# First modulation divided between TensorE and VectorE, the first squares added up on VectorE, GpSimd's products by a scalar operand

## What is computed

```python
cond = jax.nn.silu(c)
for i in range(DEPTH):
    shift, scale, gate = jnp.split(cond @ ada_w[i] + ada_b[i], 3, axis=-1)
    h = rmsnorm(x, norm_g[i]) * (1 + scale[:, None, :]) + shift[:, None, :]
    ...                       # MLA, windowed or sparse attention of h
    x = x + gate[:, None, :] * y
```

## Time and profile before

| what | us |
|---|---|
| median of 3 runs | 3254.95 (3248.53 to 3257.18) |
| the profiled execution, its own time | 3258.99 |
| its span, first to last instruction | 3257.2 |
| TensorE busy | 3047.1 (94%) |
| VectorE busy | 996.4 (31%) |
| ScalarE busy | 643.2 (20%) |
| GpSimd busy | 884.9 (27%) |
| share of TensorE in the chain that ended last | 88% |

### The profile page before, as it was taken

How to read it: one execution, slowest core, us unless ns; L and a number is a source line. 1 busy time by engine, 2 the same in 40 slices (tenths; PEclk the granted TensorE clock), 3 DMA queues, 4 the chain that set the end, 5 groups by cost and what they waited for, 6 DMA issues and landing times.

```text
span 3257.2 us, 28075 instructions
## 1 busy us (share of the span) xinstructions
PE 3047.1 (94%) x10359; PEld 1693.3 (52%) x10359; DVE 996.4 (31%) x2032; ACT 643.2 (20%) x1452; POOL 884.9 (27%) x574
## 2 busy tenths in 40 slices
PE   8899989999999998998788978999999999999997
PEld 7465555575666644554456556444444444444443
DVE  2333354324455623335544254200000222100001
ACT  1232123222233412323323122100000100100000
POOL 5480480076350008406700000381000570000000
PEclk6999999989999999998899989999999999999999
DMA  6341341153231024223200200352222442222222
GB/s 220 99 144 62 110 136 39 54 155 106 71 91 33 14 79 138 88 72 101 77 17 13 59 6 26 116 169 89 77 71 72 152 157 65 68 74 76 78 71 70
DMA packets 267621, 278.08 MB, mean 85 GB/s; under 512 B 39379, under 2 KB 240352, under 8 KB 267392
## 3 DMA queue, kind: packets, MB, share of 16 engines
q1 hardware_dynamic: 238528, 175.56, 17.8%
q0 software_dynamic: 28224, 100.86, 9.9%
q10 hardware_dynamic: 768, 0.30, 0.0%
HBM read 274.59 MB, written 2.10 MB: 85 GB/s over the span
## 4 chain that ended last, share of the span: by engine, by line
PE 88%; DVE 7%; ACT 2%; DMA 2%; issue 1%; SPq 0%; DVEq 0%; ACTq 0%
PE psum L680 44%; PE psum L825 10%; PE psum L1277 9%; PE psum L1112 2%; PE psum L707 2%; PE psum L799 2%; PE psum L1143 2%; PE psum L1098 2%; PE psum L754 2%; PE psum L722 2%; PE psum L811 1%; PE psum L1148 1%; PE psum L949 1%; PE psum L950 1%; DVE probs L2012 1%
## 5 line engine op out<-in xcount | busy, mean ns | idle before, releaser
L680 PE MATMUL psum<-h,ring 128*128 128x512 f32 (+1 forms) x3216 | 1390.1, 593 | 28.8 <-ACT h L1412 27.1
L680 PEld LDWEIGHTS psum<-h,ring 128*128 128x128 f32 x3216 | 616.4, 193 | 764.4 <-issue 749.9
L607 POOL DMA_DIRECT2D ada_ring<-in_ada_w x192 | 113.0, 588 | 1775.8 <-DVE gains L1897 1504.2
L623 POOL TENSOR_TENSOR ada_sum<-ada_sum,ada_ring 128x1024 f32<-128x1024 f32 x168 | 396.9, 2363 | 14.1
L825 PE MATMUL psum<-og,ring 128*128 128x512 f32 x768 | 333.1, 593 | 2.3 <-DVE og L2430 2.0
L619 POOL TENSOR_TENSOR ada_ring<-ada_ring,cond 128x1024 f32<-128x1024 f32 x168 | 320.0, 1905 | 4.5 <-POOL ada_sum L623 1.6
L1277 PE MATMUL psum<-arena,ring 128*128 128x512 f32 x704 | 302.5, 592 | 0.0
L825 PEld LDWEIGHTS psum<-og,ring 128*128 128x128 f32 x768 | 144.6, 190 | 181.8 <-issue 178.3
L1277 PEld LDWEIGHTS psum<-arena,ring 128*128 128x128 f32 x704 | 133.8, 190 | 168.4 <-issue 168.4
L2440 DVE TENSOR_TENSOR arena<-psum,arena 128x512 f32 x44 | 30.4, 692 | 573.8 <-PE psum L680 573.8
L2059 DVE SCALAR_TENSOR_TENSOR x<-psum,mods,x 128x512 f32<-128x512 f32 x64 | 48.1, 751 | 481.3 <-PE psum L1277 272.2
(11 more groups left out here) (285 smaller groups left out, 2793.6 us busy)
## 6 DMA issues: line engine op xcount, KB each, us to landing
ada_ring<-in_ada_w POOLq DMA_DIRECT2D x192, 512.0 KB, 4.1
ring<-in_ffn_w_gate SPq DMA_DIRECT2D x22, 1024.0 KB, 5.3
ring<-in_ffn_w_up SPq DMA_DIRECT2D x22, 1024.0 KB, 5.3
ring<-in_ffn_w_down SPq DMA_DIRECT2D x32, 704.0 KB, 4.6
ring<-in_sc_w_in SPq DMA_DIRECT2D x12, 1024.0 KB, 6.1
ring<-in_mla_w_in SPq DMA_DIRECT2D x10, 1024.0 KB, 5.4
ring<-in_mla_w_out SPq DMA_DIRECT2D x8, 1024.0 KB, 5.2
ring<-in_swa_w_in SPq DMA_DIRECT2D x16, 512.0 KB, 5.2
```

What stands on the lines that cost most here:

```text
L607: pool.dma_start(ada_ring[:, i % 2, :], w[k * P:(k + 1) * P, first(part)]).then_inc(arrived[i % 2], n.give(f"ada_in{i % 2}", 16))
L623: step = nc.gpsimd.tensor_tensor(total, total, piece, ALU.add)
L680: m = pe.matmul(tile.at[:, part], lhs(k), rhs(k), start=(k == 0), stop=(k == K - 1))
```

## The change

It touches the start, and one instruction of GpSimd's later jobs:

- TensorE computes only weight tiles 1, 4 and 7 by one-column matmuls. Tiles 0, 2, 3, 5 and 6 are multiplied by `cond` and added up over the eight steps on VectorE (`first_sums`), into the still unused `ada_sum[:, 0:2048]`; each finished tile is summed over the partitions by TensorE with one matmul per column (`column_sums`), behind all direct tiles.
- GpSimd waits for all five sums of VectorE before its first fetch.
- The squares of `x` are added on VectorE between the copies (`add_square`), as in the later blocks; TensorE has two matmuls with ones behind the row groups in place of eight between the transposes.
- VectorE runs `normed(0)` before the rotary angle, and ScalarE the root and the shifts before the sines.
- GpSimd multiplies with `tensor_scalar` by a per-partition scalar in place of `tensor_tensor` with a broadcast operand, in all 192 steps.

```diff
+FIRST_ON_PE = (1, 4, 7)
...
             pool.wait_ge(S["cond_ready"], 1)
+            pool.wait_ge(S["first_summed"], FIRST_SLOTS - len(FIRST_ON_PE))
...
-                    step = nc.gpsimd.tensor_tensor(piece, ada_ring[:, i % 2, :], c.broadcast_to([P, CHUNK]), ALU.mult)
+                    step = nc.gpsimd.tensor_scalar(piece, ada_ring[:, i % 2, :], c, None, ALU.mult)
...
-                for i in range(FIRST_SLOTS):
+                for i in FIRST_ON_PE:
                     pe.wait_ge(S[f"first_in{i}"], 16)
                     for c in range(2):
                         for k in range(KT):
-                            m = pe.matmul(tile.at[:, 2 * i + c:2 * i + c + 1], w8(first_slots[i], P * c)(k), cond[:, k:k + 1],
-                                          start=(k == 0), stop=(k == KT - 1))
-                m.then_inc(S["tile_done"], 1)
+                            pe.matmul(tile.at[:, 2 * i + c:2 * i + c + 1], w8(first_slots[i], P * c)(k), cond[:, k:k + 1],
+                                      start=(k == 0), stop=(k == KT - 1))
+                summed = [i for i in range(FIRST_SLOTS) if i not in FIRST_ON_PE]
+                for at, i in enumerate(summed):
+                    pe.wait_ge(S["first_summed"], at + 1)
+                    column_sums(tile, (2 * i, 2 * i + 1), at == len(summed) - 1)
...
             for k in range(KT):
                 turn_in(x_tok, TT, k)
-                if k:
-                    sum_squares(k - 1, first=(k == 1))
-            sum_squares(KT - 1)
             pe.wait_ge(S["rows_in"], 16 * len(late_rows))
             for g in range(1, len(ROW_GROUPS)):
                 turn_rows(g)
+            result_squares(None)
             first_columns()
...
-            for k in range(KT):
-                evacuated(next_tile())
-                square(x[:, k * T:(k + 1) * T], k)
+            squares_of_x()
             skip(len(ROW_GROUPS) - 1)
+            skip(1)
+            act.wait_ge(S["consts_in"], 16)
+            root_of_squares()
+            shift(0)
             act.wait_ge(S["sin_in"], 1)
             nc.scalar.activation(rope[:, 1, :], angle, ACT.Sin)
             nc.scalar.activation(tmp[:, 1, :], angle, ACT.Sin, scale=0.5).then_inc(S["sin_done"], 1)
-            skip(1)
-            act.wait_ge(S["consts_in"], 16)
-            root_mean_square()
-            shift(0)
...
+            def add_square(k, given):
+
+                if k > 1:
+                    dve.wait_ge(S["sum_step"], n.now("sum_step"))
+                dve.wait_ge(S["square_given"], given + k + 1)
+                nc.vector.tensor_tensor(sq_sum[:, :], sq_sum[:, :], sq[:, k % 2, :], ALU.add
+                                        ).then_inc(S["sum_step"], n.give("sum_step"))
+
+            def first_sums(i):
+
+                dve.wait_ge(S[f"first_in{i}"], 16)
+                total = ada_sum[:, 256 * i:256 * i + 256]
+                w = first_slots[i].rearrange("p (k n) -> p k n", k=KT)
+                settle(nc.vector.tensor_scalar(total, w[:, 0, :], cond[:, 0:1], None, ALU.mult))
+                for k in range(1, KT):
+                    step = nc.vector.scalar_tensor_tensor(total, w[:, k, :], cond[:, k:k + 1], total, ALU.mult, ALU.add)
+                    if k < KT - 1:
+                        settle(step)
+                step.then_inc(S["first_summed"], n.give("first_summed"))
+
             copy_rows(0)
             for k in range(KT):
                 copy_tile(x[:, k * T:(k + 1) * T])
+                if 2 <= k:
+                    add_square(k - 1, 0)
...
+            dve.wait_ge(S["cond_ready"], 1)
+            for i in range(FIRST_SLOTS):
+                if i not in FIRST_ON_PE:
+                    first_sums(i)
+            normed(0)
             dve.wait_ge(S["consts_in"], 16)
             dve.wait_ge(S["bcast_in"], 16 * 5)
             settle(nc.vector.tensor_copy(angle, pos_i))
...
             settle(nc.vector.tensor_scalar(rope[:, 0, :], tmp[:, 0, :], -2.0, 1.0, ALU.mult, ALU.add))
-            normed(0)
             mla(0)
```

More of the change, by code:

```diff
@@ L341, in build @@
         RB = psum[:, 4, :]
-        NAMES = ["ident_in", "consts_in", "cond_rows_in", "rows_in", "x_in", "bcast_in", "ctx_in", "mask_rows_zero", "rows_clean", "slot_full0", "slot_full1", "slot_begun", *(f"first_in{i}" for i in range(FIRST_SLOTS)),
+        NAMES = ["ident_in", "consts_in", "cond_rows_in", "first_summed", "rows_in", "x_in", "bcast_in", "ctx_in", "mask_rows_zero", "rows_clean", "slot_full0", "slot_full1", "slot_begun", *(f"first_in{i}" for i in range(FIRST_SLOTS)),
                  "tile_done", "tile_used0", "tile_used1", "cols_ready", "cond_ready", "ada_in0", "ada_in1",
@@ L1466, in squares_of_result, with squares_of_x @@
                 nc.scalar.activation(table_load[:, :], C["eps"], ACT.Sqrt)
+                squares_of_x()
+                root_of_squares()
+            def squares_of_x():
                 steps = n.of["sum_step"].at
@@ L1477, in squares_of_result, with root_of_squares @@
                 n.take("sum_step", KT - 2)
+            def root_of_squares():
                 act.wait_ge(S["sum_done"], n.take("sum_done"))
@@ L2493, in _ @@
                 copy_tile(x[:, k * T:(k + 1) * T])
+                if 2 <= k:
+                    add_square(k - 1, 0)
+            n.take("square_given", KT - 1)
             for g in range(1, len(ROW_GROUPS)):
                 copy_rows(g)
+            dve.wait_ge(S["cond_ready"], 1)
[3 more added lines that the diff above has]
+            normed(0)
             dve.wait_ge(S["consts_in"], 16)
```

## The result

| what | us |
|---|---|
| median after (4 runs) | 3227.67 (3221.02 to 3231.91) |
| median before beside it (4 runs) | 3253.88 (3248.53 to 3257.18) |
| ratio | 0.9919, 95% interval 0.9897 to 0.9941 |
| the profiled execution after, its own time | 3228.80 |
| its span | 3226.9 |

The change gains 26 us by the medians. The two profiled executions differ by 30.3 us in span, and the trace says where: TensorE reaches the gate columns 17.3 us earlier, and the other 13 us appear behind them, where I had reckoned with nothing. (The gate columns are the 16 one-column passes that turn GpSimd's first sum into the first block's gate.)

A forecast was written before the change was run, and what follows sets the result against it. TensorE's 51.70 us of one-column passes, mostly at 1.2 GHz, bound the start. `h` 28.2 us earlier, less 10.4 at the angle and 2.3 for the clock, put the gate columns 15 us earlier: 3240 us from 3254.95, range 3226 to 3250.

The forecast's parts named there:

- Squares and start of the direct tiles: At the start, VectorE adds the squares between copies and TensorE does two ones matmuls, done at 27.5 us.
- Last tile: Weight loads at the start: with GpSimd not fetching, the last tile lands up to 6.8 us earlier, at 41.
- Rival B: Start: last tile lands at 47.7 as before, or the angle takes 24.5 us; gain 5 to 10 us, chance 18%.
- VectorE's five tiles: VectorE's weighted sums at the start: 4.1 us a tile, 20.4 for five, from 24.0 to 44.4 us.
- Rival C: VectorE's sums: multiply-adds with both inputs in SBUF take twice 0.48 us or more; slower kernel, chance 5%.
- TensorE's tiles and `h`: Start: 20.6 us for three direct tiles, 4.3 for ten summed columns; `h` at 52.9 for 81.15, 28.2 gained.
- The angle: Rotary angle on VectorE, now behind `h`: 19.7 us beside GpSimd, delaying TensorE's third product, 10.4 us given back.
- part 6: GpSimd's first eight steps, multiply kept at 1.91 us: done at 90 to 95, hidden before the gate columns at 97.1.
- rival A: Start: angle takes only 8 to 10 us, GpSimd sets the gate columns; gain 21.6 to 28, 3227 to 3234, chance 32%.
- In the later jobs 0 to 2 us: GpSimd's jobs behind the gate columns: its multiply lies in waits, 0 to 2 us gained through fewer blocked VectorE instructions.
- Clock: TensorE's products behind its stand at the angle: lower clock makes the first take 9.3 for 6.8, 2.3 us more.
- Signs that I named: Trace signs of error: third-product wait under 3 us, GpSimd releasing the gate, late last tile, later time changed over 3.

The follow-up runs named there:

- no_pool_wait: Changed kernel without GpSimd's wait for VectorE's five sums before its first fetch: 3221.71 us, ratio 0.9865 to the kernel before.
- no_wait_2: Changed kernel without GpSimd's wait for VectorE's sums, run again in another group: 3217.25 us, ratio 0.9862 to the kernel before.
- after_tt: Changed kernel with GpSimd's multiply put back to tensor_tensor with a broadcast operand: 3244.89 us, ratio 0.9966 to the kernel before.
- before_ts: Kernel before with only GpSimd's multiply changed to tensor_scalar by a per-partition scalar: 3243.65 us, ratio 0.9965 to the kernel before.
- slow_tt: Changed kernel with GpSimd's broadcast tensor_tensor multiply, half the product then multiplied by ones in steps with an add: 3232.20 us, ratio 0.9902 to before.

## Why the prediction was right or wrong

The forecast was 3240 with a range of 3226 to 3250; 3227.67 lies in the range, at its lower end. The direction is right, and the mechanism of the start is right up to `h`. But 12 us of gain were not foreseen, and that the time lies in the range all the same is luck: the range was drawn from different places of the gate columns, with 2 us at most for everything behind them. With the measured start alone (13.8 us to the product behind the gate) the sum gives 3241, close to the forecast; the rest came from a part that the forecast had at 0 to 2 us.

- **Squares and start of the direct tiles**: 24.31 for a forecast of 27.5. A pair of copy and add takes 1.20 and not 1.46, since in this row they overlap by 0.08 us (0.68 long, begun 0.60 apart) where I had allowed a gap each, and the two ones matmuls took 2.7 and not 3.4 to 3.8.
- **Last tile**: forecast 41. The view of L473's DMAs:

```profile
L473 SPq DMA_DIRECT2D arena<-in_ada_w x2: 2807/3096/3385, 26.2 to 29.6; - x2
DMA to landing us min/median/max: 10.8/11.1/11.4
```

  29.6 + 10.8 = 40.4 for 47.7 before, 7.3 us. With GpSimd back on the queues TensorE could begin this tile at 45.60 (`no_pool_wait`) and 47.06 (`no_wait_2`) in place of 40.43, so 5 to 7 us are its absence. Rival B's first half fell.
- **VectorE's five tiles**: 3.96 us each for a forecast of 4.1, through at 42.7 for 44.4. Two SBUF inputs at 256 columns cost 0.52 a step. Rival C's price of twice that isn't there.
- **TensorE's tiles and `h`**: 6.8 to 7.0 a tile and 4.41 for the ten columns, as reckoned (6.9 and 4.3); of the 3.2 us of earlier start 2.3 went into the two load waits of 1.15 and 1.17. `h` at 52.20 for 52.9: 28.95 us gained where I said 28.2.
- **The angle**: forecast 22.8 us from the end of `h` to the end of the first copy, so 22.1 to its start; measured 15.0 to the start (57.48 to 72.49), and a stand of 4.09 for 10.4. The reckoning took over the holds of the broadcast multiply. With that multiply, in `after_tt`, it is 23.2 us and 11.36: the step itself was nearly right, for the instruction that the change had removed.
- **GpSimd's multiply, part 6**: this is the step that failed. I kept 1.91 us for `tensor_scalar`, with bounds of 0.5 and 3.8; it is 2.85. Eight steps of 6.2 to 6.5 end at 95.06 where I had 90 to 95, so the gate columns wait for GpSimd, while TensorE is there at 89: rival A's order of events, though at 95 and not between 84 and 91. That the total also falls among A's 3227 to 3234 is chance, since A has nothing behind the gate. What the bound did not carry is that duration and hold are two different sizes, the one larger and the other smaller than in the row.
- **What a page would have made of it**: by the Trainium skill (GPSIMD Engine Reference, "Engine selection") one-input work runs roughly at line rate, and the multiply would have been near 1 us, as an estimate. The trace has 2.85 us, more than the 1.91 of the two-input form. The 3 us that I gave to it did not come in that way.
- **"In the later jobs 0 to 2 us"**: the largest miss, in the sentence after. The same operand alone, in `before_ts`, gains 10.9 us, and nothing waits for GpSimd in its start. I looked at the waits of 102.83 us and concluded that GpSimd's speed can't matter there. Being faster does not help, but how it disturbs the others counts, by its holds on VectorE and, it seems, its claims on the DMAs; being slower helped. I had priced GpSimd's slack and not its neighbours.
- **Clock**: I added 2.3 us for the products behind the stand. The two took 15.67, which is 2.1 over two of 6.8. What I had not priced was the same effect at the gate: 1.65 + 1.88 = 3.5 us. It lies behind the point at which I had said that everything is decided.
- **Signs that I named**: "the wait stands at the gate columns with GpSimd as releaser" and "the time behind the gate columns changes by more than 3" both came, and rightly pointed at what was wrong. TensorE's wait before the third product, forecast at about 10, came out at 4.09, between the forecast and the 3 that was to mean rival A.

My first explanation of the 13 us was chance between executions. `before_ts` and `after_tt` with ten and twelve runs ended that. The next, the lock alone, fell with `slow_tt`. What stands is that a longer step of GpSimd's helps and that the new multiply holds VectorE for a shorter time; how the gain divides between the two is an estimate, and which of the stages carries how much is read from single executions and stays open.

## What to carry to other kernels

An instruction on an idle engine has three prices: its length, how long it holds a neighbour off, and how fast it lets the next transfer begin. Price a replaced instruction by a run of that very form, in both directions, before the sum rests on it; and if an engine has slack, try it slower. Read a gain at the first point where both kernels are again in the same state, clock included: at the gate columns the operand's start looked 4 us better, two steps later it was level. When a change removes a wait, find the wait next in line in the same trace: here two stands lay one behind the other; taking away the first alone showed no gain, the second alone 9 us, the second after the first 19.5 us.

## What the hardware showed that was not expected

- GpSimd, fp32, 128 x 1024: `tensor_scalar` with a per-partition scalar takes 2.85 us, `tensor_tensor` with a broadcast operand 1.91, the add of two tensors 2.35. The first holds VectorE off for about 1.0 us (all 38 additions of two SBUF inputs that it held; of ten 512 wide `tensor_scalar` that began later six were held to its end), the others for nearly their whole length.
- A GpSimd that does more work made the kernel faster: 168 additional instructions of 1.0 to 1.4 us, 7.5 us less in the median.
- After a stand of 6 us TensorE's 16 passes of one column took 3.57 us and the next four 3.76, against 1.92 and 1.88 without the stand; the granted clock is 0.50 in the one and 1.00 in the other.
- The kernels with the broadcast multiply spread over 17 to 21 us in twelve runs, after and its relatives over 3 to 13 us in four to six; but `before_ts`, with the scalar operand, over 18 us in ten, so the operand isn't shown to be the cause.
